# One step for two norms: final norm of the first block and first norm of the second, in halves of the tokens

## The chip, the cores and the metric
The kernel runs on one core of one Trainium2 chip. The metric is the device time of one execution in microseconds, given as the median of several runs. A profiled execution, recorded by the hardware profiler, stands beside them. In it, PE is the matrix engine, DVE the vector engine, ACT the activation engine, POOL the general engine, and SP the engine that issues most transfers.

## The reference, cut to what matters
A sequence of 256 tokens with 1024 features passes through two blocks. The first ends with an expert-choice feed-forward part (16 experts, 32 tokens each) and a norm with a gain. The second begins with a second norm, without a gain of its own in the norm, followed by a scale and a shift per feature.

```python
# end of the first block
x = x + expert_choice_ffn(h, ...)
x = rms_norm(x, final_g)              # x / sqrt(mean(x^2) + 1e-6) * final_g
# start of the second block
h = modulate(rmsnorm(x, g_pre_mix), sh1, sc1)   # rmsnorm(x) * g_pre_mix * (1 + sc1) + sh1
q, k, v, z, gl = split_proj(h @ w_in)
...
x_new = x + gt1 * rmsnorm(y, g_post_mix)        # x, the first norm's result, is needed again here
```

Put m for the mean of x squared, n for the mean of (x final_g) squared, and e for 1e-6. The second norm's factor on x final_g is then 1 / sqrt(m + e) / sqrt(n / (m + e) + e), which is 1 / sqrt(n + e m + e e).

## The kernel before, in words
The tokens are two halves of 128, `a` = 0 and 1, with one token in each partition; `X[:, a, :]` holds 1024 features of each. All engines run programs written out by hand, in order, and wait for one another by named events. `ORDER`, a list written by `mixer_order` (line 224), gives the order of the second block's stages, and each engine does its own part of each stage, where it has one.

The experts run in a loop over `e` (line 582). Each loads 24 MB of weights in twelve transfers of 2 MB on SP's queue, which goes around six buffers; PE waits for each. The last step of an expert (line 626) multiplies its 128x512 result into four banks of PSUM, `YB`, two per half of the tokens, and after the sixteenth this sum is added to `X` (line 1073, four additions on DVE). The row `final_g` and then the second block's weights follow on the same queue.

The two norms follow, half after half. ACT squares the rows and sums them up (`row_square`, line 1374), DVE forms the mean (`rstd1`, line 827), ACT takes the root (line 1371), DVE the reciprocal (`rstd2`, line 831), and one DVE instruction multiplies x by this and by `final_g` (line 1081). Then the same steps run for the second norm, ending in `XN` (`rows_normed`, line 837). Both halves go through all of this before DVE turns to the stages in `ORDER`.

`norm_turn` is such a stage: PE transposes eight 128x128 blocks of `XN` into two banks (`turn`, line 365), and DVE multiplies by the scale column (`scaled`, line 844) and adds the shift column (line 849), one bank of four blocks after the other, into `HT`. `kq` is a token group: eight products of 128x512 over the features in `HT` (`tokens`, line 375; each is two instructions of PE). The order is `norm_turn` 0, `kq` of k 0 for half 0, `norm_turn` 1, `kq` of k 0 for half 1, then the transposes of the rotated keys (`rope`, line 652), and so on, one token group after another. ACT copies raw results (line 1515), DVE rotates them (lines 1091 to 1101).

Of the kernel before, what the change touches and what calls it, by code (L numbers as in the profile page):

```python
# [121 lines left out]
def build(nc, D, out):  # L122
    from contextlib import ExitStack
    ctx = ExitStack()
    with ctx:
# [4 lines left out]
        banks = Banks()  # L130
# [29 lines left out]
        def small(n):  # L160
            taken[0] += n
            assert taken[0] <= 336
            return SM[:, taken[0] - n:taken[0]]
# [1 line left out]
        ss1, ssc, ssa, ss2, lm, ss3, ss4 = small(2), small(2), small(2), small(2), small(4), small(2), small(2)  # L165
        COL = small(64).rearrange("p (q j) -> p q j", q=8)
        lam, lamj, ssx, smv = small(4), small(128), small(2), small(8)
        LSUM, SSO, sub8, ssy, ss5, ss6 = small(32), small(16), small(8), small(4), small(2), small(2)
        lamc = lam[:, 2:3]


# [181 lines left out]
        def tensor(pe, w):  # L353
            banks.start()

            def turn(by, tag, src, strided, a, *after):
                for q in range(2):
                    b, before = banks.use(by, tag, a, q)
                    w.wait_ge(*before)
                    for event in after:  # L360
                        w.wait_ge(*event)
                    for jj in range(4):
                        j = 4 * q + jj
                        s = src[:, j::8] if strided else src[:, j * 128:(j + 1) * 128]
                        i = pe.transpose(PS[:, b, jj * 128:(jj + 1) * 128], s, ident)  # L365
                    i.then_inc(*w.hit("mm", by, tag, a, q))

            def tokens(group, key, src, a, after, used):
                b, before = banks.use(*group)
                w.wait_ge(*before)  # L370
                w.wait_ge("in", *key)
                for event in after:
                    w.wait_ge(*event)
                for j in range(8):
                    i = pe.matmul(PS[:, b, :], src[:, j, a * 128:(a + 1) * 128], IN[key][:, j, :], start=(j == 0), stop=(j == 7))  # L375
                i.then_inc(*w.hit("mm", *group, also=[("used", *key)] if used else ()))

# [204 lines left out]
            for e in range(16):  # L582
# [37 lines left out]
                for a in range(2):  # L620
                    for dc in range(2):
                        y = YB[2 * a + dc]
                        if e == 0:
                            _, before = banks.use("x2", a, dc, at=y)
                            w.wait_ge(*before)
                        x = pe.matmul(PS[:, y, :], GE[:, r, dc, a * 128:(a + 1) * 128], EO[:, r, :], start=(e == 0), stop=(e == 15),  # L626
                                      skip_group_check=True)
                x.then_inc(*w.hit("mm", "y", e))
                if e == 2:
                    context_turned()  # L630
# [4 lines left out]


            banks.ids = list(range(8))
            h2m = [[("turned", "h3", a, q) for q in range(2)] for a in range(2)]

            def norm_turn(a):  # L640
                turn("scaled", "h3", XN[:, a, :], True, a, ("xn4", a), ("col",))

            def kq(x, n, a):
                tokens(("raw", x, n, a), ("w_in2", 2 + n if x == "k" else n), HT, a, h2m[a], a == 1)

            def rope(x, n, a):
                b, before = banks.use("kq", x, n, a)
# [174 lines left out]
        def vector(v, w):  # L822

            def rstd1(tag, dst, src, n, eps, *after):
                for event in after:
                    w.wait_ge(*event)
                v.tensor_scalar(dst, src, 1.0 / n, eps, MULT, ADD).then_inc(*w.hit("mean", tag))

            def rstd2(tag, dst):
                w.wait_ge("root", tag)  # L830
                v.reciprocal(dst, dst).then_inc(*w.hit("rstd", tag))
# [4 lines left out]
                w.wait_ge("rstd", (tag, a))  # L836
                v.tensor_scalar(XN[:, a, :], X[:, a, :], ss, None, MULT).then_inc(*w.hit(name, a))  # L837

            def scaled(tag, dst, a, scale, bias, wide=128):
                for q in range(2):  # L840
                    d = dst[:, 4 * q:4 * q + 4, :]
                    b = banks.at("scaled", tag, a, q)
                    w.wait_ge("mm", "scaled", tag, a, q)
                    v.tensor_tensor(d, PS[:, b, :].rearrange("p (j t) -> p j t", j=4),  # L844
                                    scale[:, 4 * q:4 * q + 4].unsqueeze(2).broadcast_to([128, 4, 128]), MULT).then_inc(
                        *w.hit("scaled", tag, a, q))
                    if bias is not None:
                        w.wait_ge("scaled", tag, a, q)
                        v.tensor_tensor(d, d, bias[:, 4 * q:4 * q + 4].unsqueeze(2).broadcast_to([128, 4, 128]), ADD).then_inc(  # L849
                            *w.hit("turned", tag, a, q))  # L850
# [196 lines left out]
            for e in range(16):  # L1047
# [18 lines left out]
                elif e == 2:  # L1066
                    for a in range(2):
                        scaled("hc", HCT[:, :, a * 128:(a + 1) * 128], a, COL[:, 1, :], COL[:, 6, :])
            w.wait_ge("mm", "y", 15)
            for a in range(2):  # L1070
                for dc in range(2):
                    x = X[:, a, dc * 512:(dc + 1) * 512]
                    v.tensor_tensor(x, x, PS[:, YB[2 * a + dc], :], ADD).then_inc(*w.hit("x2", a, dc))


            for a in range(2):
                rstd1(("x3", a), ss3[:, a:a + 1], ss3[:, a:a + 1], 1024, 1e-6, ("sumsq", "x3", a))
                rstd2(("x3", a), ss3[:, a:a + 1])
                w.wait_ge("in", "final_g")
                w.wait_ge("rstd", ("x3", a))  # L1080
                v.scalar_tensor_tensor(X[:, a, :], X[:, a, :], ss3[:, a:a + 1], IN["final_g",], MULT, MULT).then_inc(
                    *w.hit("x3", a, also=[("used", "final_g")] if a else ()))
                w.wait_ge("x3", a)
                rows_normed("x4", a, ss4[:, a:a + 1], "xn4")

            def rope(x, n, a):
                r = a
# [250 lines left out]
            def leave(a):  # L1338
# [4 lines left out]
                for m in range(2):  # L1343
# [12 lines left out]
            mine = {"rope": rope, "zn1": zn1, "zn2": zn2, "zn3": zn3, "zmix": zmix, "ga": ga, "gs": gs, "bs": bs, "exp": att_exp,  # L1356
                    "cmb": att_combine, "gain1": lambda: row_of("g1", G1, COL[:, 3, :]), "gain2": lambda: row_of("g2", G2, COL[:, 4, :]),
                    "hn1": hn1, "hn2": hn2, "ht": heads_turn, "bae": bae, "ope": ope, "up1": up1, "up2": up2, "fn1": fn1, "fn2": fn2,
                    "norm_turn": lambda a: scaled("h3", HT[:, :, a * 128:(a + 1) * 128], a, COL[:, 0, :], COL[:, 5, :]),
                    "ft": ffn_turn, "rt0": rt0, "rt1": rt1, "rt2": rt2, "rt3": rt3, "rt4": rt4, "row": row, "rt5": rt5, "leave": leave}  # L1360
            for stage, *x in ORDER:
                if stage in mine:
# [4 lines left out]
        def scalar(act, w):  # L1367
# [132 lines left out]
                        act.copy(VC[:, a, n * 512:(n + 1) * 512], PS[:, banks.at("vc", n, a), :]).then_inc(*w.hit("vc", n, a))  # L1500


            for a in range(2):
                w.wait_ge("x2", a, 1)
                row_square("x3", a, ss3[:, a:a + 1])
                root(("x3", a), ss3[:, a:a + 1])
                w.wait_ge("x3", a)
                row_square("x4", a, ss4[:, a:a + 1])
                root(("x4", a), ss4[:, a:a + 1])

            def kq(x, n, a):
                w.wait_ge("mm", "raw", x, n, a)
# [123 lines left out]
            def leave(a):  # L1636
# [4 lines left out]
                for m in range(2):  # L1641
# [1 line left out]
                                   accum_out=SMX[:, a, 2 + m:3 + m]).then_inc(*w.hit("sumsq", "out", a, m))  # L1643
                root(("out", a), SMX[:, a, 2:3])

            mine = {"rope": rope, "vals": vals, "z": z, "zn1": zn1, "zn2": lambda: root("zv", smv[:, 4:6]), "zturn": zturn, "ga": ga, "gs": gs,
                    "exp": att_exp, "cmb": att_combine, "trn": att_turn, "ao": att_out,
                    "hn1": lambda a: root(("on", a), SSO[:, a * 8:a * 8 + 8]), "yt": lambda a: copied("yt", YT, a), "ope": ope,
                    "up1": lambda a: root(("y2", a), ss5[:, a:a + 1]), "up2": up2, "fn1": lambda a: root(("x5", a), ss6[:, a:a + 1]),
# [247 lines left out]
```

## Time and profile before
| | us |
|---|---|
| median of 3 runs | 2269.64 |
| lowest and highest | 2269.09, 2276.59 |
| the profiled execution | 2265.3 |
| its span | 2263.2 |
| PE busy | 1522.1 |
| DVE busy | 754.9 |
| ACT busy | 421.1 |
| POOL busy | 291.4 |

Busy time is added up over the whole span, and no engine is busy for all of it: the first two thirds are the experts, where the weights come in at some 427 GB/s, then comes the second block's mixer, where PE works and transfers are few, and then a search and gather of rows, where transfers are many again. The granted clock is given as a share of full speed, 1.00 being 2.4 GHz and 0.50 being 1.2 GHz.

### The profile page before, as it was taken

How to read it: one execution, taken by the hardware profiler on the slowest of the kernel's cores; microseconds unless marked ns; L12 is line 12 of the kernel's file. 1: busy time of each engine (PE TensorE's matmuls, PEld its weight loads, DVE VectorE, ACT ScalarE, POOL GpSimd, SP SyncE). 2: the span in 40 equal slices, each digit the busy share in tenths (PEclk: the TensorE clock that was granted, in tenths of full speed). 3: DMA queues.
4: the chain of work that ended last, by engine and by line, in shares of the span. 5: the costliest groups of instructions: out<-in, count | busy, mean ns of one | idle time of the engine just before them, and what ended most of it. 6: DMA issues, size and time to landing. Idle time of an engine off the chain costs nothing.

```text
span 2263.2 us, 24573 instructions
## 1 busy us (share of the span) xinstructions
PE 1522.1 (67%) x10304; PEld 635.3 (28%) x10304; DVE 754.9 (33%) x1895; ACT 421.1 (19%) x975; POOL 291.4 (13%) x265
## 2 busy tenths in 40 slices
PE   8999766677776566566658999876565754434433
PEld 7556211222221111111114445445323420101000
DVE  5823001000000000000013132245666677776774
ACT  1321100000000000000011154153233332323221
POOL 0000000000000000000000000002334344435341
PEclk9987878778988887888879999988786875655555
DMA  9548899999999999999983331317999999999996
GB/s 377 192 180 334 354 426 427 426 427 427 427 427 427 427 427 427 427 426 428 428 363 145 147 149 75 149 75 291 425 425 378 410 416 417 421 422 422 423 423 276
DMA packets 74238, 797.26 MB, mean 352 GB/s; under 512 B 8208, under 2 KB 8336, under 8 KB 9232
## 3 DMA queue, kind: packets, MB, share of 16 engines
q1 hardware_dynamic: 37264, 527.24, 55.8%
q0 software_dynamic: 36864, 268.45, 28.5%
q8 instruction: 81, 1.33, 0.2%
q14 instruction: 29, 0.24, 0.0%
HBM read 794.62 MB, written 1.05 MB: 352 GB/s over the span
## 4 chain that ended last, share of the span: by engine, by line
DMA 46%; PE 32%; DVE 12%; ACT 4%; POOL 4%; issue 2%; POOLq 0%; ACTq 0%; DVEq 0%
DMA AR<-in_w_down 19%; DMA AR<-in_w_up 15%; PE PS L375 12%; DMA AR<-in_peer_uv,AR 12%; POOL AR L1671 4%; DVE AR L1324 3%; PE PS L596 2%; PE PS L386 2%; PE PS L614 2%; PE PS L755 2%; PE PS L797 2%; PE PS L488 1%; DVE AR L874 1%; DVE AR L876 1%; PE PS L626 1%
## 5 line engine op out<-in xcount | busy, mean ns | idle before, releaser
L1671 POOL DMA_INDIRECT AR<-in_peer_uv,AR x256 | 289.6, 1131 | 1762.0 <-PE PS L712 1380.3
L797 PE MATMUL PS<-AR 32*32 32x512 f32 x4096 | 231.6, 938 | 338.3 <-ACT AR L1633 338.2
L596 PE MATMUL PS<-AR 128*32 128x512 f32 x2048 | 310.0, 743 | 187.7 <-DMA AR<-in_w_up 125.1
L1324 DVE CUSTOM_DVE_ANT_0 AR<-AR 128x1024 f32<-128x1024 f32 x256 | 309.3, 1222 | 161.7 <-DMA AR<-in_peer_uv,AR 161.7
L375 PE MATMUL PS<-AR 128*128 128x512 f32 x736 | 328.8, 602 | 8.3 <-DVE AR L849 7.9
L614 PE MATMUL PS<-AR 128*32 128x512 f32 x1024 | 179.0, 836 | 104.2 <-DMA AR<-in_w_down 96.6
L1053 DVE TENSOR_TENSOR AR<-AR,PS 128x512 f32<-128x512 f32 x16 | 11.0, 688 | 606.1 <-PE PS L596 606.1
L375 PEld LDWEIGHTS PS<-AR 128*128 128x128 f32 x736 | 138.8, 193 | 178.3 <-issue 175.4
L596 PEld LDWEIGHTS PS<-AR 128*32 128x32 f32 x2048 | 64.0, 123 | 422.2 <-DMA AR<-in_w_up 204.4
L797 PEld LDWEIGHTS PS<-AR 32*32 32x32 f32 x4096 | 44.0, 127 | 481.6 <-ACT AR L1633 469.6
L1061 DVE COPY AR<-PS 128x512 f32<-128x512 f32 x16 | 11.1, 692 | 288.9 <-PE PS L614 288.9
L614 PEld LDWEIGHTS PS<-AR 128*32 128x32 f32 x1024 | 33.6, 133 | 232.7 <-DMA AR<-in_w_down 154.2
L386 PE MATMUL PS<-AR 128*128 128x256 f32 x384 | 85.6, 386 | 0.9 <-DVE AR L844 0.9
L1475 ACT ACTIVATE AR<-PS 128x512 f32<-128x512 f32 x16 | 9.6, 597 | 400.4 <-PE PS L596 400.4
L386 PEld LDWEIGHTS PS<-AR 128*128 128x128 f32 x384 | 74.4, 194 | 12.6 <-issue 2.2
L626 PE MATMUL PS<-AR 128*128 128x512 f32 x128 | 66.6, 669 | 14.4 <-DVE AR L1061 14.4
L1627 ACT ACTIVATE AR<-AR 128x2 f32<-128x2 f32 x128 | 25.7, 201 | 242.1 <-DVE AR L1324 241.6
L755 PE MATMUL PS<-AR 128*128 128x128 f32 x512 | 69.5, 301 | 0.8 <-ACT PS L1583 0.8
L1633 ACT ACTIVATE AR<-AR 128x32 f32<-128x32 f32 x256 | 68.3, 314 | 9.2 <-ACT AR L1627 0.4
L755 PEld LDWEIGHTS PS<-AR 128*128 128x128 f32 x512 | 67.0, 215 | 10.3 <-issue 10.3
L1479 ACT COPY AR<-PS 128x512 f32<-128x512 f32 x16 | 9.4, 585 | 318.5 <-PE PS L603 318.5
L365 PE MATMUL PS<-PK,AR 128*128 128x128 f32 x128 | 23.9, 351 | 29.8 <-DVE AR L837 11.1
(257 smaller groups left out, 1280.2 us busy)
## 6 DMA issues: line engine op xcount, KB each, us to landing
AR<-in_w_gate SPq DMA_DIRECT2D x64, 2048.0 KB, 26.0
AR<-in_w_up SPq DMA_DIRECT2D x64, 2048.0 KB, 25.9
AR<-in_w_down SPq DMA_DIRECT2D x64, 2048.0 KB, 26.5
AR<-in_w_in SPq DMA_DIRECT2D x23, 2048.0 KB, 9.6
AR<-in_w_ada SPq DMA_DIRECT2D x12, 2048.0 KB, 8.3
AR<-in_peer_w_query SPq DMA_DIRECT2D x8, 2048.0 KB, 10.0
AR<-in_w_out SPq DMA_DIRECT2D x6, 2048.0 KB, 11.1
AR<-in_w_branch_attn SPq DMA_DIRECT2D x4, 2048.0 KB, 9.6
```

What stands on the lines that cost most here:

```text
L365: i = pe.transpose(PS[:, b, jj * 128:(jj + 1) * 128], s, ident)
L375: i = pe.matmul(PS[:, b, :], src[:, j, a * 128:(a + 1) * 128], IN[key][:, j, :], start=(j == 0), stop=(j == 7))
L386: i = pe.matmul(PS[:, b, q * 256:(q + 1) * 256], IN[key][:, j, (e + q) * 128:(e + q + 1) * 128], src[:, j, :], start=(j == 0), stop=(j == 7))
L596: x = pe.matmul(PS[32 * q:32 * q + 32, bk, :], XS[:, j, e * 32:(e + 1) * 32], IN[key][:, jj, q * 512:(q + 1) * 512], start=(j == 0), stop= ...
L614: x = pe.matmul(PS[32 * g:32 * g + 32, b, :], HDT[:, s, fq * 32:(fq + 1) * 32], IN[key][:, s, dc * 512:(dc + 1) * 512], start=(fq == 0 and ...
L626: x = pe.matmul(PS[:, y, :], GE[:, r, dc, a * 128:(a + 1) * 128], EO[:, r, :], start=(e == 0), stop=(e == 15), skip_group_check=True)
L755: x = pe.matmul(PS[:, b, q * 128:(q + 1) * 128], IN[key][:, j, (2 * r + q) * 128:(2 * r + q + 1) * 128], HT[:, j, a * 128:(a + 1) * 128], ...
L797: x = pe.matmul(PS[c:c + 32, ACC[a][g], :], DI[t, p, r, :], AR[t, off + 1024 + m * 512:off + 1536 + m * 512], start=(h == 0 and p == 0), s ...
L1324: v.tensor_tensor_reduce(rows, rows, HB[:, a, :], 1.0, 0.0, MULT, ADD, DOT[:, ix, k:k + 1]).then_inc(*w.hit("dot", ix, k))
L1627: w.step(act.activation(two, DOT[:, ix, 2 * p:2 * p + 2], ACT.Gelu))
L1633: i = act.activation(DI[:, p, r, :], SG2[:, ix % 2, 2 * p + r, :], ACT.Copy, scale=two[:, r:r + 1])
L1671: pool.indirect_dma_start(out=AR[:, off:off + 2048], out_offset=None, in_=D["peer_uv_2"], in_offset=bass.IndirectOffsetOnAxis(ap=EI[:, ix, ...
```

## The change
The second norm's factor is taken from two sums that don't depend on the first norm's result: of x squared, and of (x `final_g`) squared. DVE forms x `final_g` in `VV` (`gained`), ACT squares both, and `both_norms` makes the factor and writes `XN`. The two halves of the tokens are taken apart: PE tells when half 0 of the experts' sum is complete, and DVE does half 0 first, with half 1's steps put between half 0's. In `norm_turn` the first bank of four blocks stays with DVE and the second goes to ACT, by Identity with scale and shift; a token group waits for the second only before its fifth product. The first norm's result, needed later as the residual, is made after the turns. A root of one column that nobody reads stands ahead of it on ACT.

```diff
@@ PE
+            def turn(by, tag, src, strided, a, *after, second=None):
+                for q in range(2):
+                    by = second if q and second else by
...
                 for j in range(8):
+                    for event in midway if j == 4 else ():
+                        w.wait_ge(*event)
                     i = pe.matmul(PS[:, b, :], src[:, j, a * 128:(a + 1) * 128], IN[key][:, j, :], start=(j == 0), stop=(j == 7))
...
+                    if (e, a) == (15, 0):
+                        x.then_inc(*w.hit("mm", "y", e, a))
                 x.then_inc(*w.hit("mm", "y", e))
...
-                turn("scaled", "h3", XN[:, a, :], True, a, ("xn4", a), ("col",))
+                turn("scaled", "h3", XN[:, a, :], True, a, ("xn4", a), second="moved")
...
-                tokens(("raw", x, n, a), ("w_in2", 2 + n if x == "k" else n), HT, a, h2m[a], a == 1)
+                tokens(("raw", x, n, a), ("w_in2", 2 + n if x == "k" else n), HT, a, h2m[a][:1], a == 1, h2m[a][1:])
@@ DVE
-            w.wait_ge("mm", "y", 15)
-            for a in range(2):
+            w.wait_ge("in", "final_g")
+
+            def block_out(a):
+                w.wait_ge("mm", "y", *((15,) if a else (15, 0)))
                 for dc in range(2):
                     x = X[:, a, dc * 512:(dc + 1) * 512]
                     v.tensor_tensor(x, x, PS[:, YB[2 * a + dc], :], ADD).then_inc(*w.hit("x2", a, dc))
-            for a in range(2):
-                rstd1(("x3", a), ss3[:, a:a + 1], ss3[:, a:a + 1], 1024, 1e-6, ("sumsq", "x3", a))
-                rstd2(("x3", a), ss3[:, a:a + 1])
-                w.wait_ge("in", "final_g")
-                w.wait_ge("rstd", ("x3", a))
-                v.scalar_tensor_tensor(X[:, a, :], X[:, a, :], ss3[:, a:a + 1], IN["final_g",], MULT, MULT).then_inc(
-                    *w.hit("x3", a, also=[("used", "final_g")] if a else ()))
-                w.wait_ge("x3", a)
-                rows_normed("x4", a, ss4[:, a:a + 1], "xn4")
+            def gained(a):
+                w.wait_ge("x2", a, 1)
+                v.tensor_tensor(VV[:, a, :], X[:, a, :], IN["final_g",], MULT).then_inc(
+                    *w.hit("xf", a, also=[("used", "final_g")] if a else ()))
+            def both_norms(a):
+                s3, s4 = ss3[:, a:a + 1], ss4[:, a:a + 1]
+                w.wait_ge("sumsq", "x3", a)
+                w.step(v.tensor_scalar(s8[:, a:a + 1], s3, 1e-6, 1e-12, MULT, ADD))
+                w.wait_ge("sumsq", "x4", a)
+                w.wait_step()
+                v.tensor_tensor(s4, s4, s8[:, a:a + 1], ADD).then_inc(*w.hit("mean", ("x4", a)))
+                rstd2(("x4", a), s4)
+                w.wait_ge("rstd", ("x4", a))
+                v.tensor_scalar(XN[:, a, :], VV[:, a, :], s4, None, MULT).then_inc(*w.hit("xn4", a))
+
+            block_out(0)
+            gained(0)
+            block_out(1)
+            both_norms(0)
+            gained(1)
+
+            def norm_turn(a):
+                scaled("h3", HT[:, :, a * 128:(a + 1) * 128], a, COL[:, 0, :], COL[:, 5, :], (0,))
+                if a == 0:
+                    both_norms(1)
+                    return
+                rstd1("x3", ss3, ss3, 1, 1e-6)
+                rstd2("x3", ss3)
+                w.wait_ge("rstd", "x3")
+                for i in range(2):
+                    v.tensor_scalar(X[:, i, :], VV[:, i, :], ss3[:, i:i + 1], None, MULT).then_inc(*w.hit("x3", i))
@@ ACT
+            def gained_square(a):
+                w.wait_ge("xf", a)
+                act.activation(QX[:, a, :, :].rearrange("p h t -> p (h t)"), VV[:, a, :], ACT.Square, scale=1.0 / 32,
+                               accum_out=ss4[:, a:a + 1]).then_inc(*w.hit("sumsq", "x4", a))
+                root(("x4", a), ss4[:, a:a + 1])
+
+            act.activation(s8[:, 2:3], ident[:, 0:1], ACT.Sqrt)
             for a in range(2):
                 w.wait_ge("x2", a, 1)
-                row_square("x3", a, ss3[:, a:a + 1])
-                root(("x3", a), ss3[:, a:a + 1])
-                w.wait_ge("x3", a)
-                row_square("x4", a, ss4[:, a:a + 1])
-                root(("x4", a), ss4[:, a:a + 1])
+                act.activation(Y[:, a, :], X[:, a, :], ACT.Square, scale=1.0 / 32, accum_out=ss3[:, a:a + 1]).then_inc(*w.hit("sumsq", "x3", a))
+                if a == 0:
+                    gained_square(0)
+
+            def norm_turn(a):
+                w.wait_ge("mm", "moved", "h3", a, 1)
+                for j in range(4, 8):
+                    i = act.activation(HT[:, j, a * 128:(a + 1) * 128], PS[:, banks.at("moved", "h3", a, 1), (j - 4) * 128:(j - 3) * 128],
+                                       ACT.Identity, scale=COL[:, 0, j:j + 1], bias=COL[:, 5, j:j + 1])
+                i.then_inc(*w.hit("moved", "h3", a, 1))
+                if a == 0:
+                    gained_square(1)
+                else:
+                    root("x3", ss3)
```

## Rows read from the trace of the kernel before

**Rows 1.** The page's chain of waits, shares of the span by engine.
```profile
DMA 46%; PE 32%; DVE 12%; ACT 4%; POOL 4%; issue 2%; POOLq 0%; ACTq 0%; DVEq 0%
```

**Rows 2.** The chain in order of time, from the last expert product: start, us, what.
```profile
1172.22 3.69 PE PS L626 x8
...
1175.93 1.29 DVE AR L1073 x2
...
1177.25 1.15 ACT AR L1374 x2
...
1178.42 1.28 ACT L1371
...
1179.71 0.21 ACT AR L1371
...
1180.21 1.29 DVE AR L1081
...
1182.78 0.17 DVE AR L827
```

**Rows 3.** The same view, up to the second token group.
```profile
1188.06 0.75 DVE AR L837
...
1189.45 0.69 DVE AR L849
...
1191.48 0.14 issue
1191.61 9.26 PE PS L375 x16
1200.87 0.45 PE PS L365 x4
...
1201.35 0.70 DVE AR L844
...
1202.08 0.69 DVE AR L849
...
1203.40 0.70 DVE AR L849
...
1204.24 7.11 PE PS L375 x16
```

**Rows 4.** Instructions in order of time: start, us, engine, line, operands.
```profile
1144.81 0.33 SPq L1694 DMA_DIRECT2D AR<-in_final_g  x1
...
1183.40 0.75 DVE L837 TENSOR_SCALAR AR<-AR 128x1024 f32<-128x1024 f32 x1
...
1184.26 1.94 PE L365 MATMUL PS<-PK,AR 128*128 128x128 f32 x8 [8.36 <-issue]
...
1186.18 25.53 SPq L1694 DMA_DIRECT2D AR<-in_w_in  x2
...
1204.01 0.69 DVE L1091 TENSOR_TENSOR AR<-AR,PK 128x512 f32<-128x512 f32 x1
...
1205.87 0.42 DVE L1101 TENSOR_TENSOR AR<-AR 128x256 f32<-128x256 f32 x1
```

**Rows 5.** Transfers issued from 1140 to 1300: KB each, median us to landing.
```profile
AR<-in_final_g SPq DMA_DIRECT2D x1, 512.0 KB, 24.1
```

**Rows 6.** Busy time in stretches: us, PE, PEld, DVE, ACT, POOL, clock, DMA, GB/s.
```profile
1178.00:1180.00 2.00, 0.00 (x0) 0.00 (x0) 0.62 (x3) 1.89 (x4) 0.00 (x0) 0.72 0.77 328
...
1184.00:1186.00 2.00, 1.74 (x8) 1.57 (x8) 1.61 (x4) 0.42 (x3) 0.00 (x0) 0.50 0.00 0
...
1196.00:1198.00 2.00, 2.00 (x6) 0.94 (x5) 0.00 (x0) 0.00 (x0) 0.00 (x0) 1.00 0.00 0
...
1230.00:1250.00 20.00, 20.00 (x57) 9.47 (x56) 4.97 (x11) 3.22 (x6) 0.00 (x0) 1.00 0.53 211
```

**Rows 7.** Two lines of the kernel: durations in ns, min, median, max; forms.
```profile
L1121 DVE TENSOR_TENSOR AR<-AR x2: 1225/1226/1226, 1339.0 to 1341.4; 128x1024 f32<-128x1024 f32 x2
...
L1435 ACT ACTIVATE AR<-AR,PK x4: 585/586/601, 105.5 to 107.0; 128x256 f32<-128x256 f32 x4
```

More of the change, by code:

```diff
@@ L167, in build @@
         lam, lamj, ssx, smv = small(4), small(128), small(2), small(8)
-        LSUM, SSO, sub8, ssy, ss5, ss6 = small(32), small(16), small(8), small(4), small(2), small(2)
+        LSUM, SSO, sub8, ssy, ss5, ss6, s8 = small(32), small(16), small(8), small(4), small(2), small(2), small(4)
         lamc = lam[:, 2:3]
@@ L354, in tensor @@
             banks.start()
-            def turn(by, tag, src, strided, a, *after):
+            def turn(by, tag, src, strided, a, *after, second=None):
                 for q in range(2):
+                    by = second if q and second else by
                     b, before = banks.use(by, tag, a, q)
@@ L366, in turn, with tokens @@
                     i.then_inc(*w.hit("mm", by, tag, a, q))
-            def tokens(group, key, src, a, after, used):
+            def tokens(group, key, src, a, after, used, midway=()):
                 b, before = banks.use(*group)
@@ L637, in tensor @@
             banks.ids = list(range(8))
-            h2m = [[("turned", "h3", a, q) for q in range(2)] for a in range(2)]
+            h2m = [[("turned", "h3", a, 0), ("moved", "h3", a, 1)] for a in range(2)]
             def norm_turn(a):
-                turn("scaled", "h3", XN[:, a, :], True, a, ("xn4", a), ("col",))
+                turn("scaled", "h3", XN[:, a, :], True, a, ("xn4", a), second="moved")
             def kq(x, n, a):
-                tokens(("raw", x, n, a), ("w_in2", 2 + n if x == "k" else n), HT, a, h2m[a], a == 1)
+                tokens(("raw", x, n, a), ("w_in2", 2 + n if x == "k" else n), HT, a, h2m[a][:1], a == 1, h2m[a][1:])
             def rope(x, n, a):
@@ L837, in rows_normed, with scaled @@
                 v.tensor_scalar(XN[:, a, :], X[:, a, :], ss, None, MULT).then_inc(*w.hit(name, a))
-            def scaled(tag, dst, a, scale, bias, wide=128):
-                for q in range(2):
+            def scaled(tag, dst, a, scale, bias, parts=(0, 1)):
+                for q in parts:
                     d = dst[:, 4 * q:4 * q + 4, :]
@@ L1358, in vector @@
                     "hn1": hn1, "hn2": hn2, "ht": heads_turn, "bae": bae, "ope": ope, "up1": up1, "up2": up2, "fn1": fn1, "fn2": fn2,
-                    "norm_turn": lambda a: scaled("h3", HT[:, :, a * 128:(a + 1) * 128], a, COL[:, 0, :], COL[:, 5, :]),
+                    "norm_turn": norm_turn,
                     "ft": ffn_turn, "rt0": rt0, "rt1": rt1, "rt2": rt2, "rt3": rt3, "rt4": rt4, "row": row, "rt5": rt5, "leave": leave}
@@ L1644, in leave @@
                 root(("out", a), SMX[:, a, 2:3])
-            mine = {"rope": rope, "vals": vals, "z": z, "zn1": zn1, "zn2": lambda: root("zv", smv[:, 4:6]), "zturn": zturn, "ga": ga, "gs": gs,
+            mine = {"norm_turn": norm_turn, "rope": rope, "vals": vals, "z": z, "zn1": zn1, "zn2": lambda: root("zv", smv[:, 4:6]), "zturn": zturn, "ga": ga, "gs": gs,
                     "exp": att_exp, "cmb": att_combine, "trn": att_turn, "ao": att_out,
```

## The prediction, made before the changed kernel ran
> **What bounds the kernel now.** I read the page's chain of waits first. No engine and no queue sets the whole length: DMA holds 46% of the chain, PE 32%, DVE 12% and ACT 4% [rows 1]. The changed place lies between the last expert and the first products of the second block, so I then read the chain there in order of time. From 1175.91 us, where PE's last expert product ends, to 1191.61, where PE starts the first token group (`kq` for k, half 0), the chain runs through DVE and ACT alone [rows 2, 3]: two additions to x (1.29 us), a Square (1.15), a load of an activation table (1.28), a square root (0.21), the gain (1.29), and then the second norm. The reader is to see that the chain goes through both halves of the tokens: the row scaling of half 1 at 1188.06 stands in front of the turn of half 0, although half 0's rows were scaled at 1183.40 and transposed from 1184.26 [rows 3, 4]. DVE simply has the second half's norms ahead of the first half's turn. So PE stands still for 15.7 us, but for eight transposes.
>
> A second gap follows: the first token group ends at 1200.87 and the next starts at 1204.24, 3.37 us in which the second half is transposed, scaled and shifted by DVE alone [rows 3].
>
> No transfer ends late here. The row of `final_g` was issued at 1144.81 and landed 24.1 us later, at about 1168.9 [rows 4, 5]. After 1204 PE is full: 20.00 us of 20.00 between 1230 and 1250 at a granted clock of 1.00 [rows 6]. What PE starts earlier here, it therefore ends earlier, and nothing later in the program starts at a time of its own.
>
> **The change, part by part.** I rebuild the path to the first token group with durations of this trace.
>
> *Start.* The eight instructions of the last expert product take 3.69 us [rows 2]. The event of half 0 now comes after four, 1.85 us earlier: 1174.07. The added wait for `final_g` stands ahead of this on DVE; it landed at 1168.9, so 5 us remain, and its price is 0.
>
> *Statistics of half 0.* Two additions, 1.29: 1175.38. Then two things run side by side. ACT squares x (1.15, to 1176.55). DVE multiplies x by the gain; the nearest row is a product of the same form, 128x1024, at 1.226 us [rows 7]: 1176.63. ACT squares that product, 1.15 again with 0.02 for the event: about 1177.82. DVE adds half 1's products meanwhile, 1.29: 1177.92, and forms e m + e e (0.17): 1178.1. So DVE, not ACT, is last, and the sum n + e m + e e follows at 1178.3 (0.17), the root at 1178.5 (0.21), the reciprocal at 1178.7 (taken as 0.17), the row scaling at 1179.5 (0.75, as the row at 1183.40 [rows 4]).
>
> The table load of 1.28 us stood on the path [rows 2] and is now provoked by the extra Sqrt of one column while ACT has nothing to do. What covers it is ACT's idle time under the last expert's products; without that cover it costs 1.28. The row shows the root starting 1.29 us after the load began. The Trainium skill (ScalarE: Activation LUTs, What ACT_TABLE_LOAD costs) adds a drain of about 1380 ns to each switch of tables, 2.66 us together; by that the sum would be 1.4 us larger, but the trace disagrees, as nothing stands between load and root, and I go by the row.
>
> *Turn of half 0.* Before, the transposes started 0.11 us after the row scaling; that gives 1179.6. Eight took 1.94 [rows 4], the first four half of that: 1180.6. DVE has the gain product of half 1 in front of the turn: from about 1179.45, 1.23 long, to 1180.7, so the two meet. Multiply (0.70 and 0.03 to the next), add (0.70), 0.14 to PE [rows 3]: the first token group starts at 1182.25. That is 9.36 us earlier than 1191.61. Only half the features are needed then; the other half is ACT's, four Identity instructions per half of the tokens. No Identity stands in the trace. The nearest above is the 128x256 Silu with two column operands, 0.586 [rows 7]: at most 2.34 for four, after 1181.6, done by 1183.9; two table loads around them would add 2.57. Below, four cost nothing, and a gain is excluded since PE waits for the other half. PE needs them at the fifth of eight products, 3.5 us after 1182.25 even at full clock. I take 0 on the path.
>
> Half 1's second Square, its root and its scaling run under the first token group: from 1184 the same steps take 1.15 + 2 x 0.17 + 0.21 + 0.17 + 0.75, to about 1187, and the group ends after 1191 if it keeps its 9.26 us. That is over 4 us of cover; without it each microsecond would count.
>
> *Second gap.* From the end of that group: four transposes 0.45, 0.02, multiply 0.70, 0.03, add 0.70, 0.14 to PE, together 2.04 where 3.37 stood [rows 3]. Gain 1.33.
>
> *What is moved behind it.* The residual x is now formed by two row scalings (2 x 0.75) ahead of the first rotation on DVE, and ACT copies the first raw keys only after its four Identities and a root. Counted from the end of the first group: transposes 0.9, Identities 2.34 at most, root 0.21, reciprocal 0.17, scalings 1.5, rotation 2.28 (1204.01 to 1206.29 [rows 4]): 7.4 us. PE comes for the rotated keys after 2.04 + 7.11 = 9.15. So 1.75 us of cover remain. On SP the load waiting for the buffer of `final_g` went out at 1186.18 [rows 4] and now can at about 1180.7; no product needs it before 1230. POOL has nothing here.
>
> **Sum.** 9.36 + 1.33 = 10.7 us. The profiled execution took 2265.3 us (span 2263.2 and 2.1 around it), which would become 2254.6. The median of the runs shown is 4.3 us above that execution, and I take the same difference from it: 2269.64 - 10.7 = 2258.9, that is -0.47%. Neighbouring DVE instructions without a dependence overlap a little, so up to 0.3 more is possible.
>
> **The clock is the open term.** The first token group took 9.26 us where the next took 7.11 [rows 3]: a granted clock of 0.50 at first, 1.00 from about 1196 [rows 6]. The clock had fallen between 1178 and 1180, some 3 us after PE's last product. In the new order the pause to the first transposes is 3.7 us instead of 8.4, so the fall comes just before them. Before, the eight transposes ran at 0.50 and left it there (0.50 in 1184 to 1186 [rows 6]), and so I keep 9.26, although they now stand close ahead of the group. The ends: 7.11 if the clock never falls or comes back at once (2.15 better), 14.2 if the whole group runs at half clock (5.0 worse).
>
> **Rivals.**
> *Clock up sooner.* The fall doesn't happen in the shorter pause, or ends early: 10.7 + 2.15 = 12.9 us, 2256.8. For it: 3.7 us of pause is close to the 3 us after which the clock fell. Against it: the fall came while PE was idle, and it is idle longer than that again.
> *Cover of the rotation lost.* The Identities bring table loads, 2 x 1.28, so that 7.4 becomes 10.0 where 9.15 is allowed: 0.8 given back, 2259.7. The Trainium skill (ScalarE: Activation LUTs, Table sets: the hidden batching unit) has identity in every table set, which speaks against it; no Identity stands in this trace.
> *Part of it lost later.* The shifted work meets one or two further falls of the clock behind 1204, at 2.15 each: about 6.4 left, 2263.2. For it: chance in where pauses fall. Against it: no waits of PE's follow soon [rows 6].
> *Slower.* The new wait in the middle of the first two token groups breaks up PE's work, and the clock stays at 1.2 GHz. The first group then costs 5.0 more and the second 7.1, which already uses up the 10.7 (+1.4); it is slower from there on, and with the third group at half clock (+6.9) the time is 2277.9. Against it: ACT is done with its half before PE gets to that wait.
>
> **Chances.** Forecast 0.60, clock up sooner 0.18, cover lost 0.06, part lost later 0.12, slower 0.04. A measurement of this kernel tells about 0.5% from no change, 11.35 us here; the forecast lies just inside. All of the second case and a good third of the first (0.24) make 0.42 for faster by over 0.5%; the slower case in its deeper half and a disturbed measurement make 0.03; 0.55 remain within. The range goes from 2253 (both good ends, and some spread of the runs) to 2266 (part lost later, and the same spread).
>
> **What would show it.** Right: the first additions start before 1174.2 on this time scale; no table load between 1174 and 1182; the first token group about 9.4 us earlier, released by DVE's add; 2.0 us between the first and second group; PE's wait in mid-group zero. Wrong: a table load around an Identity, PE waiting for ACT inside a token group, a wait of the first rotation's transposes for DVE, or a first token group far from 9.26 us.

## The result and the profile after

The changed kernel takes 2256.24 us (median; 2252.92 to 2257.76), the kernel before 2269.64: a ratio of 0.9938, interval 0.9915 to 0.9962 (estimated from all runs of both; the medians alone give 0.9941). That lies inside the range of the forecast, 2.7 us under its 2258.9. The profiled execution took 2253.5 us, with a span of 2251.4.

The chain of waits through the changed place, in order of time (start, us, what), the counterpart of [rows 2, 3]:

```profile
1166.62 3.76 PE PS L629 x4
...
1170.48 1.29 DVE AR L1080 x2
...
1171.80 1.22 DVE AR L1084
1173.02 1.20 DVE AR L1080 x2
...
1174.38 0.17 DVE AR L1096
...
1174.58 0.21 ACT AR L1403
...
1175.01 0.75 DVE AR L1099
1175.76 1.13 DVE AR L1084
1176.90 0.61 DVE AR L849
...
1177.53 0.70 DVE AR L854
...
1178.37 10.03 PE PS L378 x16
1188.40 0.45 PE PS L366 x4
...
1190.35 7.13 PE PS L378 x16
```

The chain leaves PE after four instructions of the last expert product (1170.38), and no table load and no Square stands in it any more: DVE carries it, as forecast, with half 1's additions and both gain products in it. It is a close thing: ACT's second Square ended at 1174.21, DVE's e m + e e at 1174.27. The whole last product ends at 1172.27. From there to the first token group 6.10 us pass, where it was 15.70, and between the groups 1.95 (1188.40 to 1190.35), where it was 3.37.

The instructions around it (start, us, engine, line, operands), for [rows 4]:

```profile
1149.16 1.28 ACT L1541 ACT_TABLE_LOAD   x1
...
1166.62 5.65 PE L629 MATMUL PS<-AR 128*128 128x512 f32 x8 [0.88 <-DVE AR L1066]
...
1175.91 1.12 PE L366 MATMUL PS<-PK,AR 128*128 128x128 f32 x8 [3.64 <-DVE AR L1099]
...
1177.07 1.51 ACT L1551 ACTIVATE AR<-PS,AR 128x128 f32<-128x128 f32 x4 [1.25 <-PE PS L366]
...
1178.37 10.03 PE L378 MATMUL PS<-AR 128*128 128x512 f32 x16 [1.34 <-DVE AR L854]
...
1191.16 1.42 DVE L1116 TENSOR_SCALAR AR<-AR 128x1024 f32<-128x1024 f32 x2
...
1194.35 0.42 DVE L1133 TENSOR_TENSOR AR<-AR 128x256 f32<-128x256 f32 x1
...
1197.32 0.60 PE L657 MATMUL PS<-PK,AR 128*128 128x128 f32 x4
```

The table load now runs 17 us ahead of the last expert product, while ACT has nothing to do. Four Identities take 1.51 us without a table load and are done at 1178.6, while the group asks for them in its second half. The first rotation ends at 1194.77, and PE comes for it at 1197.3.

But the two profiles differ by 11.8 us of span, and not all of that is here. The first expert product, 950 us ahead of the change (the experts take 229 to 1176 of the 2263 us, not the first two thirds), starts at 229.2 us in one and at 224.6 in the other (lines of both kernels: ns min, median, max, first and last start):

```profile
L596 PE MATMUL PS<-AR x2048: 589/593/1063, 229.2 to 1150.6; 128*32 128x512 f32 x187
```
```profile
L599 PE MATMUL PS<-AR x2048: 589/593/1063, 224.6 to 1145.9; 128*32 128x512 f32 x187
```

The code up to there is the same in both. A difference of two spans is therefore no measure of this change, and I compare a stretch instead: from the start of DVE's copy of the last expert's result to the end of the second token group. It is 39.96 us before (1171.39 to 1211.35) and 31.70 after (1165.78 to 1197.48). The copies, with the last weight chunk ahead of the first, are in the kernel before

```profile
1167.68 3.64 PE L614 MATMUL PS<-AR 128*32 128x512 f32 x16 [1.27 <-DMA AR<-in_w_down]
1171.39 0.69 DVE L1061 COPY AR<-PS 128x512 f32<-128x512 f32 x1 [18.31 <-PE PS L614]
```

and in the changed kernel

```profile
1165.78 0.69 DVE L1066 COPY AR<-PS 128x512 f32<-128x512 f32 x1 [17.42 <-PE PS L617]
```

### The profile page after: what moved, and what is told of

It is laid out like the page before. It is cut to its first block, busy times and chain, and to the rows that moved or that the text cites. A ratio compares the mean times of both kernels' runs of the same rounds, so it can differ in the third digit from the quotient of the medians.

```text
span 2251.4 us, 24577 instructions
## 1 busy us (share of the span) xinstructions
PE 1521.4 (68%) x10304; PEld 634.7 (28%) x10304; DVE 753.5 (33%) x1893; ACT 424.0 (19%) x983; POOL 295.5 (13%) x265
## 4 chain that ended last, share of the span: by engine, by line
DMA 47%; PE 31%; DVE 11%; POOL 4%; ACT 4%; issue 3%; POOLq 0%; ACTq 0%; DVEq 0%
DMA AR<-in_w_down 19%; DMA AR<-in_w_up 15%; DMA AR<-in_peer_uv,AR 13%; PE PS L378 13%; POOL AR L1719 4%; DVE AR L1356 3%; PE PS L599 2%; PE PS L617 2%; PE PS L389 2%; PE PS L760 2%; PE PS L802 2%; PE PS L491 1%; DVE AR L879 1%; DVE AR L881 1%; PE PS L629 1%
## 5 line engine op out<-in xcount | busy, mean ns | idle before, releaser
L599 PE MATMUL PS<-AR 128*32 128x512 f32 x2048 | 305.2, 733 | 187.8 <-DMA AR<-in_w_up 125.5
L378 PE MATMUL PS<-AR 128*128 128x512 f32 x736 | 330.1, 604 | 2.9 <-DVE AR L854 2.4
L617 PE MATMUL PS<-AR 128*32 128x512 f32 x1024 | 178.4, 833 | 106.1 <-DMA AR<-in_w_down 98.6
L378 PEld LDWEIGHTS PS<-AR 128*128 128x128 f32 x736 | 139.5, 194 | 173.2 <-issue 171.6
L1066 DVE COPY AR<-PS 128x512 f32<-128x512 f32 x16 | 11.1, 692 | 290.6 <-PE PS L617 290.6
L629 PE MATMUL PS<-AR 128*128 128x512 f32 x128 | 70.7, 703 | 14.4 <-DVE AR L1066 14.4
L389 PEld LDWEIGHTS PS<-AR 128*128 128x128 f32 x384 | 72.9, 190 | 12.0 <-issue 2.2
L760 PEld LDWEIGHTS PS<-AR 128*128 128x128 f32 x512 | 68.3, 218 | 9.8 <-issue 9.8
L629 PEld LDWEIGHTS PS<-AR 128*128 128x128 f32 x128 | 27.7, 228 | 65.5 <-issue 65.5
## 6 DMA issues: line engine op xcount, KB each, us to landing
AR<-in_w_out SPq DMA_DIRECT2D x6, 2048.0 KB, 11.1
```

The source lines that it names most:

```text
L389: i = pe.matmul(PS[:, b, q * 256:(q + 1) * 256], IN[key][:, j, (e + q) * 128:(e + q + 1) * 128], src[:, j, :], start=(j == 0), stop=(j == 7))
L599: x = pe.matmul(PS[32 * q:32 * q + 32, bk, :], XS[:, j, e * 32:(e + 1) * 32], IN[key][:, jj, q * 512:(q + 1) * 512], start=(j == 0), stop= ...
L617: x = pe.matmul(PS[32 * g:32 * g + 32, b, :], HDT[:, s, fq * 32:(fq + 1) * 32], IN[key][:, s, dc * 512:(dc + 1) * 512], start=(fq == 0 and ...
L760: x = pe.matmul(PS[:, b, q * 128:(q + 1) * 128], IN[key][:, j, (2 * r + q) * 128:(2 * r + q + 1) * 128], HT[:, j, a * 128:(a + 1) * 128], ...
```

## The experiments

For all of them, read from the profiles: "pause" from the end of the last expert product to the first token group, "group" the first token group, "gap" from its end to the second, in us. The ratio is to the kernel before in the same comparison.

| | ratio, interval | pause | group | gap |
|---|---|---|---|---|
| kernel before | | 15.70 | 9.26 | 3.37 |
| changed kernel | 0.9938, 0.9915 to 0.9962 | 6.10 | 10.03 | 1.95 |
| rep_before | 0.9995, 0.9984 to 1.0005 | 15.72 | 10.17 | 3.36 |
| again_before | 1.0008, 0.9992 to 1.0023 | 15.74 | 9.26 | 3.36 |
| rep_after | 0.9939, 0.9921 to 0.9957 | 6.28 | 9.84 | 1.95 |
| again_after | 0.9942, 0.9920 to 0.9963 | 6.29 | 9.85 | 1.95 |
| no_root | 0.9933, 0.9912 to 0.9955 | 7.36 | 9.31 | 1.94 |
| one_engine | 0.9943, 0.9924 to 0.9963 | 7.61 | 9.10 | 3.36 |
| no_halves | 0.9954, 0.9938 to 0.9971 | 10.39 | 9.46 | 1.94 |
| formula_only | 0.9990, 0.9975 to 1.0005 | 12.71 | 10.11 | 3.36 |
| warm | 0.9913, 0.9897 to 0.9929 | 6.28 | 7.11 | 1.94 |
| before_warm | 0.9990, 0.9978 to 1.0003 | 15.72 | 7.10 | 3.37 |
| warm_weights | 0.9923, 0.9905 to 0.9941 | 6.30 | 7.11 | 1.94 |
| delay | 0.9985, 0.9971 to 0.9999 | 17.62 | 9.25 | 1.95 |

**The same two kernels again.** No edit.

> The kernel before once more, for what a second profile of the same program differs by. In the first pair of profiles the changed kernel began its first expert product at 224.57 us and the kernel before at 229.15, 4.6 us apart, in code that the change doesn't touch. Theory A (the difference is where the granted clock happens to rise and fall, anew in each execution): the ratio is 1.000 within 0.2%, and in the new profile the first expert product starts anywhere from 223 to 230. Theory B (the change moved something ahead of its place): it starts within 0.5 us of 229.15 again. Both: from the end of the last expert product to the first token group 15.7 us, between the two token groups 3.4.

> The changed kernel once more. Theory A: ratio 0.993 to 0.9955, near the 10.7 us (0.9953) that the changed place can give, rather than the 13.4 of the first comparison; the first expert product again starts anywhere from 223 to 230. Theory B: ratio 0.994 or less, and the first expert product starts within 0.5 us of 224.57. Both: 6.1 us from the last expert product to the first token group, 1.95 between the groups, first group 7.1 to 11 by the clock.

The first expert product starts at 226.5 us in this second profile of the kernel before and at 229.1 in that of the changed kernel, so its place belongs to the execution and not to the change: theory B falls. Pauses and gaps repeat within 0.2 us. What varies in the changed place is what runs at a clock: the last product and the first group. The kernel before, second profile (PE in order of time):

```profile
1169.51 5.30 PE L626 MATMUL PS<-AR 128*128 128x512 f32 x8 [0.91 <-DVE AR L1061]
1183.18 1.95 PE L365 MATMUL PS<-PK,AR 128*128 128x128 f32 x8 [8.37 <-issue]
1190.53 10.17 PE L375 MATMUL PS<-AR 128*128 128x512 f32 x16 [5.40 <-DVE AR L849]
```

and the changed kernel, second profile, with the last weight chunk and the first additions:

```profile
1167.33 1.92 PE L617 MATMUL PS<-AR 128*32 128x512 f32 x16 [1.66 <-DMA AR<-in_w_down]
...
1170.16 3.67 PE L629 MATMUL PS<-AR 128*128 128x512 f32 x8 [0.91 <-DVE AR L1066]
1172.22 1.29 DVE L1080 TENSOR_TENSOR AR<-AR,PS 128x512 f32<-128x512 f32 x2 [2.21 <-PE PS L629]
...
1177.65 1.12 PE L366 MATMUL PS<-PK,AR 128*128 128x128 f32 x8 [3.83 <-DVE AR L1099]
1180.11 9.84 PE L378 MATMUL PS<-AR 128*128 128x512 f32 x16 [1.34 <-DVE AR L854]
```

But the ratio came out at 0.9939 once more. That is inside the 0.993 to 0.9955 written down, but not near the 0.9953 that the changed place can give and that I had expected.

**Without the early root.** `-act.activation(s8[:, 2:3], ident[:, 0:1], ACT.Sqrt)`

> The changed kernel without the root of one column that nobody reads. My theory: the table load of 1.28 us stands between the second Square and the first root again, the first token group starts 1.3 us later after the last expert product, 7.4 in place of 6.1, and the time rises by 1.3 us (0.06%), too little to see in the ratio. The rival, that a switch of tables costs 2.66 us with a drain: 8.8 in place of 6.1.

The load stands on the path again, and the root follows it at once (the changed kernel without the root, in order of time):

```profile
1174.11 1.28 ACT L1403 ACT_TABLE_LOAD   x1
1174.28 0.16 DVE L1096 TENSOR_TENSOR AR<-AR 128x1 f32<-128x1 f32 x1
1175.41 0.20 ACT L1403 ACTIVATE AR<-AR 128x1 f32<-128x1 f32 x1
```

The pause is 7.36 us, as forecast, and the rival's 8.8 is not seen: the root starts 0.02 us after the load's end. In the ratio 1.3 us can't be seen either way.

**Both banks of a turn on DVE.**
```diff
...
-                turn("scaled", "h3", XN[:, a, :], True, a, ("xn4", a), second="moved")
+                turn("scaled", "h3", XN[:, a, :], True, a, ("xn4", a))
...
-                scaled("h3", ..., COL[:, 5, :], (0,))
+                scaled("h3", ..., COL[:, 5, :])
...
```

> The changed kernel with both banks of each turn scaled and shifted by DVE again, and each token group waiting for both. By the rows of before a bank is 1.30 to 1.33 us of DVE. My theory: the first token group starts 1.3 us later after the last expert product (7.4 for 6.1), the gap between the groups is 3.4 for 1.95, and the time is 2.6 to 2.8 us above the changed kernel. The rival, that ACT's half was never what the groups waited for and the gain comes from the norms alone: both distances stay within 0.3 us of those of the changed kernel.

Pause 1.3 to 1.5 us longer, gap 3.36: the second engine is worth 1.4 us in each of the two places, as forecast from the 1.3 of a bank. The median is 1.6 us above that of rep_after, in another comparison; the two ratios, 0.9943 and 0.9939, can't tell such a difference.

**The halves joined.**
```diff
-                w.wait_ge("mm", "y", *((15,) if a else (15, 0)))
+                w.wait_ge("mm", "y", 15)
...
             block_out(0)
-            gained(0)
             block_out(1)
-            both_norms(0)
+            gained(0)
             gained(1)
+            both_norms(0)
+            both_norms(1)
...
```

> The changed kernel with the halves of the tokens joined again: one event of PE for the expert sum, both additions, both gain products and both norms ahead of the first turn; the one-step formula, the two engines in the turn and the early root stay. Theory A by rows: the additions start with the end of the last expert product (2 to 2.8 us later), half 1's additions, gain product and norm stand ahead of the turn (1.2 and some 1.5 us); the first token group starts 10 to 11 us after the last expert product for 6.1, and the time is 4 to 5 us above the changed kernel, 9 under the kernel before. The rival, that the one-step formula alone brings nearly all: 7 us or less, and the time within 1.5 us of the changed kernel.

The kernel with the halves joined, in order of time:

```profile
1170.79 3.67 PE L629 MATMUL PS<-AR 128*128 128x512 f32 x8 [0.91 <-DVE AR L1066]
1174.57 2.48 DVE L1080 TENSOR_TENSOR AR<-AR,PS 128x512 f32<-128x512 f32 x4 [3.92 <-PE PS L629]
...
1184.85 9.46 PE L378 MATMUL PS<-AR 128*128 128x512 f32 x16 [1.89 <-DVE AR L854]
```

The pause is 10.39 us, so the halves are worth 4.1; the ratio, 0.9954, agrees in direction (the median is 3.2 us above that of rep_after). Two things make up the 4.1, as rep_after shows, whose last product also took 3.67 us. The additions start 3.78 us after the start of that product here and 2.06 there, so the early event is worth 1.7. From the additions to the first group it is 10.28 us here and 7.89 there, so the order of the steps is worth 2.4.

**The formula alone.** The edits of no_root, one_engine and no_halves together.

> The one-step formula alone: halves joined, both banks of a turn on DVE, no early root. By rows: 10.4 us from the last expert product to the first token group with the halves joined, 1.3 more for the table load and 1.3 more for the second bank on DVE, so 13.0, and 3.5 between the groups: 2.6 us less than before, to 2270.5 if the kernel before is at 2273. Theory D (the 3 to 4 us that the comparisons show beyond the changed place come with the formula, which all variants tried share): 5.5 to 7 us less than the kernel before. Theory E (they come with the halves, the second engine or the shift together, or were chance): 1.5 to 3.5 us less.

The formula alone (PE in order of time):

```profile
1169.73 5.58 PE L629 MATMUL PS<-AR 128*128 128x512 f32 x8 [0.88 <-DVE AR L1066]
...
1188.02 10.11 PE L378 MATMUL PS<-AR 128*128 128x512 f32 x16 [3.21 <-DVE AR L854]
```

12.71 and 3.36: the formula by itself takes 3.0 us out of the pause, and the comparison shows 0.9990, some 2 us, not told from nothing (0.9975 to 1.0005). The parts add up: 3.0 for the formula, 1.1 to 1.3 for the early root, 4.1 for the halves, 1.3 in the pause and 1.4 in the gap for the second engine are 10.9 to 11.1, where the whole change shows 9.4 to 9.6 and 1.4. This speaks against theory D, that what exceeds the changed place comes with the formula alone: its 5.5 us and more lie at the far end of the interval.

**PE kept at work in the pause.**
```diff
+            def busy(n, bank):
+                for _ in range(n):
+                    pe.matmul(PS[:, bank, :], ident, pk("swT")[:, 0:512], start=True, stop=True)
+            busy(3, BG)
             def norm_turn(a):
                 turn("scaled", "h3", XN[:, a, :], True, a, ("xn4", a), second="moved")
+                busy(1 - a, (banks.n + 5) % 8)
```

> The changed kernel, with three more products of PE right behind the last expert product and one between the transposes of half 0 and the first token group, into banks that nobody reads; they change no result. My theory, the clock as the open term: PE's pause of 3.6 us costs half clock in the first token group; with PE at work in the pause the clock stays where it is, the first group takes 7.1 to 7.3 us in place of 10.03, and the time falls by 2 to 3 us against the changed kernel; if the last expert product itself runs at half clock, the clock comes up during the added products. The rival, that half clock in the first group is carried over from the weights' end of the experts and not from the pause: the group stays at 9 to 10 us and the time stays the same, or rises by up to 1 us where the added products stand in the way of the transposes.

PE in order of time in this kernel; line 647 is the added products:

```profile
1169.84 5.31 PE L629 MATMUL PS<-AR 128*128 128x512 f32 x8 [0.90 <-DVE AR L1073]
1174.98 2.74 PE L647 MATMUL PS<-PK 128*128 128x512 f32 x6
1178.97 1.12 PE L366 MATMUL PS<-PK,AR 128*128 128x128 f32 x8 [1.25 <-DVE AR L1106]
1179.92 1.02 PE L647 MATMUL PS<-PK 128*128 128x512 f32 x2
1181.43 7.11 PE L378 MATMUL PS<-AR 128*128 128x512 f32 x16 [0.48 <-DVE AR L861]
```

The clock in the same stretch, with and without the added products (columns as in [rows 6]; the clock is the third number from the end). With them:

```profile
1178.00:1180.00 2.00, 1.03 (x9) 1.06 (x10) 1.97 (x4) 0.88 (x2) 0.00 (x0) 1.00 0.36 156
1180.00:1182.00 2.00, 1.52 (x5) 0.48 (x5) 1.31 (x3) 1.87 (x5) 0.00 (x0) 1.00 0.65 156
1182.00:1184.00 2.00, 2.00 (x6) 0.89 (x5) 1.00 (x3) 0.87 (x3) 0.00 (x0) 1.00 0.91 377
```

Without them, in the changed kernel:

```profile
1176.00:1178.00 2.00, 1.03 (x8) 0.84 (x8) 1.97 (x3) 0.93 (x3) 0.00 (x0) 0.86 0.48 147
1178.00:1180.00 2.00, 1.63 (x2) 0.84 (x3) 0.45 (x3) 1.77 (x5) 0.00 (x0) 0.50 0.81 262
...
1184.00:1186.00 2.00, 2.00 (x5) 0.76 (x4) 0.00 (x0) 0.00 (x0) 0.00 (x0) 0.93 0.04 16
```

The group takes 7.11 us, and the rest of the place is unchanged: the pause is what costs the clock. The median is 2252.28 us, 5.0 under rep_after. The group explains 2.7 to 2.9 of that, as the theory had it; the intervals of the two ratios overlap, so the rest is not told. By the medians this kernel and `warm_weights`, below, are the fastest of all that ran.

**The same for the kernel before.** Eight products and five, at the same places.
```diff
...
+            busy(8, BG)
...
             def norm_turn(a):
                 turn("scaled", "h3", XN[:, a, :], True, a, ("xn4", a), ("col",))
+                busy(5 - 5 * a, (banks.n + 5) % 8)
```

> The kernel before, with eight more products of PE behind the last expert product and five between the transposes of half 0 and the first token group, into banks that nobody reads; they change no result. It takes the clock out of the comparison: its partner is the changed kernel with PE kept at work in the same way (2252.3 us). Theory A (the change saves 11.0 us of steps, and what was measured beyond that is clock in the pause): the first token group takes 7.1 us where it took 9.3 and 10.2, the time is 2 to 3 us under the kernel before, and the partner lies 11 us under it. Theory C (some 3 us more are saved behind or ahead of the changed place): the partner lies 14 us or more under it. Both: 15.7 us from the last expert product to the first token group.

The group takes 7.10 us, and the ratio is 0.9990, about 2.3 us (0.9978 to 1.0003). The clock is thus out of both, pause and gap differ by 9.4 and 1.4, 10.9 in all, and the partner, `warm`, lies some 17 us lower by the two ratios (0.9913 and 0.9990). Theory A's 11 us are not enough here, and theory C's 14 or more are met.

**PE kept at work under the last weights too.** One product behind each of the first three weight chunks of the last expert, `if e == 15 and fq < 3: busy(1, BG)`.

> The changed kernel with PE kept at work in the pause, and one more product behind each of the first three weight chunks of the last expert. It tells what the clock costs ahead of the changed place: the last expert product took 3.7 us in some profiles and 5.3 to 5.65 in others, and the last weight chunk 1.9 or 3.65. My theory: the clock comes up before the last chunk, both run at full clock (1.9 and 3.7 us) and the time falls by 1 to 3 us against 2252.3. The rival, that products of 32 columns keep the clock down in any case: both stay at 3.65 and 5.3, and the time stays or rises by up to 0.5 us.

Last chunk 1.92 us and last product 3.67, but two of three profiles of the changed kernel have these without any help, and the median, 2252.75, is that of `warm`. It decides nothing.

**The turn held back.** Nine DVE additions of 128x1024 ahead of the turn of half 0.
```diff
             def norm_turn(a):
+                for _ in range(9 - 9 * a):
+                    w.step(v.tensor_tensor(U[:, 0, :], VV[:, 0, :], VV[:, 0, :], ADD))
+                    w.wait_step()
```

> The changed kernel with nine more DVE instructions of 128x1024 ahead of the turn of half 0, which write a buffer that is overwritten later: the first token group starts 11.2 us later (9 times about 1.25) and all the rest of the program is the changed kernel's. Open so far: the changed place gives 10.5 to 11 us in the profiles, the comparisons of times 14 to 16. Theory C1 (what runs behind, and where the clock falls there, depends on when it starts): the time rises by 14 to 16 us and is the kernel before's, 2271. Theory C2 (the excess has to do with the changed code and not with the shift): the time rises by 11 us, to 2268, 3 us under the kernel before.

PE in order of time in this kernel:

```profile
1172.05 5.37 PE L629 MATMUL PS<-AR 128*128 128x512 f32 x8 [0.90 <-DVE AR L1066]
1181.24 1.12 PE L366 MATMUL PS<-PK,AR 128*128 128x128 f32 x8 [3.83 <-DVE AR L1099]
1195.04 9.25 PE L378 MATMUL PS<-AR 128*128 128x512 f32 x16 [12.67 <-DVE AR L854]
```

Pause and gap together are 0.5 us longer than in the kernel before (17.62 + 1.95 against 15.72 + 3.36), and yet the ratio is 0.9985 (0.9971 to 0.9999), 3.4 us less. The time rose by 11.5 us against the changed kernel in the same comparison (2271.11 and 2259.58), which is the delay itself and not the 14 to 16 us of C1. C1 falls. C2 holds as far as it goes, with an interval that ends at 0.9999.

**Once more both.** No edit.

> The kernel before a third time, for a further profile and more times. If the excess of 3 to 5 us over the changed place is real, then some stretch of unchanged code is longer in the profiles of before than in those of the changed kernel by that much: from the start to the first expert product (226.5 to 229.2 so far), from the second token group to the first scores (75.8 and 78.8), from the last scores to the first gathered row (44.8 and 46.7), or over the gathered rows (670.3 to 674.8). If each stays inside its values in the changed kernel's profiles (224.6 to 229.6; 75.8 to 77.6; 44.8 to 46.6; 668.3 to 675.6), no stretch can be named.

> The changed kernel a third time, beside the kernel before on the same chip: ratio 0.9935 to 0.9945 if the excess is real and lasting, 0.9950 to 0.9955 if the first comparisons were 3 us off by chance. Same stretches as for the kernel before.

The ratio is 0.9942, inside what was written down for a lasting excess. In the profile of before, the first expert product starts at 228.5 us, and the other stretches of the list too lie inside what the profiles of the changed kernel and its variants show. One stretch is not in that list: the experts themselves, from the first expert product to DVE's copy of the last result. They take 942.2 us in each of the three profiles of the kernel before, and 941.2, 940.3 and 940.2 in those of the changed kernel, 1.6 less on the mean. The last weight chunk alone took 3.64 us in each of the former and 2.8, 1.92 and 1.92 in the latter. The code is the same there, and either program shows both (`before_warm` 940.2; `warm` 942.2, `delay` 942.1), so this isn't shown to come with the change.

## Why the prediction was right, and where not

*Start of half 0.* Right in kind: the additions begin behind the fourth instruction of the last product. But they start 2.06 us after the product's start where it took 3.67 (1170.16 to 1172.22), not 1.85: in the chain of that profile four of the eight instructions take 1.97 us to end, and 0.09 more pass. By the forecast's time scale they start at 1174.3, just behind its sign of 1174.2. Before, they started 0.04 after the product's end (1175.89 to 1175.93), so the early event gained 1.65 us and not 1.85, and 1.8 in the profile above, where the first four instructions ran at half clock.

*Statistics, root and turn.* Right: 9.36 us were forecast for the pause, and the three profiles of each kernel give 9.6, 9.4 and 9.4. Part of this agreement is luck: the 0.2 us lost at the start are made up by some 0.3 behind it, where 8.18 us were reckoned from the additions to the group and 7.89 passed. The forecast had allowed up to 0.3 for overlap of neighbouring DVE instructions. The order of what is late was right too: DVE, with the second gain product directly in front of the turn.

*Second gap.* 2.04 forecast, 1.95 measured.

*Covers.* The Identities came at 0.38 us each, without table loads, which is what the Trainium skill (ScalarE: Activation LUTs, Table sets: the hidden batching unit) would have; the trace agrees, with 1.51 for four. The rotation ended 6.4 us after the first group where 7.4 was reckoned, and PE came 2.55 us after that. No wait of PE's for ACT stands inside a group.

*The clock.* This is the term that was mis-sized. I kept 9.26 us for the first group; it took 10.03, 9.84 and 9.85, and before 9.26, 10.17 and 9.26, so the means are 0.3 us apart, the changed kernel's being the longer; the three values of before differ by more than that. The detail was wrong too: the transposes still ran at full clock (1.12 us for eight, not 1.94), and the clock fell just behind them, before the group. DVE hid the difference, since it was busy with the gain product. The rival "clock up sooner" did not happen, though the time, 2256.2, is nearly the one that it named: its group was to be 7.11 us.

*Part of it lost later.* The rival said that the shifted work might meet a further fall of the clock, and the case against it was that no waits of PE's follow soon. One does follow, in both kernels: PE waits 3.57 us for a rotation on DVE, some 51 us behind the second group. Before, with the 48 instructions behind it:

```profile
1266.06 0.63 PE L652 MATMUL PS<-PK,AR 128*128 128x128 f32 x4 [3.57 <-DVE AR L1101]
1266.53 20.77 PE L375 MATMUL PS<-AR 128*128 128x512 f32 x48
```

and the same 48 in the changed kernel:

```profile
1252.78 22.34 PE L378 MATMUL PS<-AR 128*128 128x512 f32 x48
```

In the changed kernel the granted clock falls just behind that wait (0.57 from 1252 to 1256 here, and 3.4 us at half clock in each of its three profiles); from the second group to the first scores each takes 77.6 us. The kernel before takes 75.9, 78.8 and 75.9: its clock falls there in one profile of three. So something of this rival happened, 1.7 us in each profile, but not shown to be the change's doing, as the kernel before lost more there in one of its profiles.

*The sum.* For the whole stretch, copy to end of second group, the three profiles of before give 39.96, 42.49 and 39.97, those of the changed kernel 31.70, 29.71 and 29.73: means of 40.8 and 30.4, so 10.4 us where 10.7 was forecast. The comparisons of times give more: 0.9938, 0.9939 and 0.9942, about 13 to 14 us. Each interval contains 10.4 (0.9954), but all three lie on the same side, and `warm` against `before_warm` as well as `delay` against the kernel before point to 3 us or more that are not in the stretch. The runs speak against the shift in time (`delay`), the clock in the pause (`before_warm`) and the formula by itself (`formula_only`) as its cause. It shows in the variants with halves or with the second engine (one_engine 0.9943, no_halves 0.9954, where pause and gap give 0.9964 and 0.9970, at the upper end of the interval of each or just past it). In the profiles it is smaller: the mean spans, 2267.0 and 2255.4, are 11.6 us apart, the 10.4 of the stretch and 1.6 in the experts' unchanged code, less 0.7 behind the second group, with 0.3 in sum elsewhere. Where these 3 us come from, or whether three comparisons were off to one side, stays open: the unchanged code around the stretch varies by 7 us and more between profiles of one kernel, and they don't settle it.

## What to carry to other kernels

Where two halves go through a chain of small steps on two engines, ask what the waiting engine needs first, and in which order the engine that carries the chain has it. Taking the halves apart was worth more here (4.1 us) than the shorter formula (3.0): 2.4 for half 1's steps behind half 0's, 1.7 for starting half 0 before half 1's product was done. To measure a change of 10 us in an execution of 2260, compare the stretch between two events around it in several profiles: the spans of one kernel differ by as much. The pause of PE cost twice here, once as the pause and once as half clock in the group behind it (9.84 to 10.03 us for 7.11), and a few products that nobody reads gave the second part back.

## What the runs showed of the hardware

The same program, same inputs, has its first expert product at 224.6, 226.6 and 229.1 us in three profiles, and its first token group at 9.84 to 10.03 us; both go with the clock. In the one at 229.1, PE, busy nearly throughout, got 12 instructions done from 14 to 18 us where the others got 20 and 21, and from 100 to 224 us the mean granted clock was 0.85 in the one at 224.6 and 0.82 in the other two; the group's time goes by where the clock rises in it. Three products of 128x512 in a pause of 3.8 us, and one more ahead of the group, kept the clock at 1.00 through 1.3 us of rest. Eight transposes, after 3.6 to 3.8 us of rest, did not: the clock fell right behind them (0.50 from 1178 to 1180). Why is not shown.
